# Two orders changed in the opening of a two-block transformer kernel: VectorE's first wait, and what TensorE does between two sets of transposes

## The reference, cut to what matters

```python
for l in range(DEPTH):                       # two layers
    h = rmsnorm(x, g_mix_pre[l])
    mk, mv = jnp.split(rmsnorm(mem, g_mem[l]) @ w_mem_kv[l], 2, axis=-1)
    ...
```

## Time and profile before

| | before |
|---|---|
| median of 3 runs | 2247.61 us (2244.99 to 2247.92) |
| the profiled execution's own time | 2242.63 us |
| its span, first to last instruction | 2241.2 us |
| TensorE, matmuls | 2093.4 us busy, 93% |
| VectorE | 1163.9 us busy, 52% |
| ScalarE | 867.2 us busy, 39% |
| GpSimd | 233.6 us busy, 10% |
| mean granted TensorE clock | 0.97 |

### The profile page before, as it was taken

One profiled execution on the slowest core, in us unless ns is written; L12 is line 12 of the kernel. 1 busy time (PEld: TensorE's weight loads), 2 busy tenths in 40 slices (PEclk: granted clock), 3 DMA queues, 4 the chain that ended last, 5 costly groups with the idle time before them and its releaser, 6 DMA issues.

```text
span 2241.2 us, 24583 instructions
## 1 busy us (share of the span) xinstructions
PE 2093.4 (93%) x9984; PEld 1703.9 (76%) x9984; DVE 1163.9 (52%) x2252; ACT 867.2 (39%) x1553; POOL 233.6 (10%) x161
## 2 busy tenths in 40 slices
PE   6988899999998899999999998999999799999787
PEld 6976688888786777688887888877777566877675
DVE  5325453333225756553333226998964528766553
ACT  5345443222124356532223122367552223256520
POOL 1000010000002000010000002677700000000000
PEclk9999899999999999999999999999999899999998
DMA  6320122232223112223222222222222222211211
GB/s 229 113 91 4 48 85 94 94 101 106 96 102 113 58 65 85 85 85 106 101 94 94 94 104 103 94 76 76 94 86 94 75 75 76 76 38 38 75 57 56
DMA packets 28800, 192.60 MB, mean 86 GB/s; under 512 B 3264, under 2 KB 3408, under 8 KB 7440
## 3 DMA queue, kind: packets, MB, share of 16 engines
q1 hardware_dynamic: 24848, 175.96, 22.5%
q0 software_dynamic: 3264, 12.99, 1.7%
q10 hardware_dynamic: 576, 2.10, 0.2%
HBM read 186.84 MB, written 4.19 MB: 85 GB/s over the span
## 4 chain that ended last, share of the span: by engine, by line
PE 79%; DVE 14%; ACT 5%; issue 1%; DMA 0%; POOL 0%; SPq 0%; DVEq 0%; ACTq 0%; POOLq 0%
PE bank L397 23%; PE bank L398 22%; PE bank L399 22%; DVE bank L2064 5%; PE bank L1750 2%; DVE WL L369 2%; PE bank L1738 1%; PE bank L1641 1%; ACT WH L355 1%; PE bank L1651 1%; PE bank L2205 1%; PE bank L1212 1%; DVE XL L558 1%; PE bank L1743 1%; PE bank L542 1%
## 5 line engine op out<-in xcount | busy, mean ns | idle before, releaser
L397 PE MATMUL bank<-XH,WH 128*128 128x512 f32 (+1 forms) x1504 | 597.1, 397 | 15.7 <-DVE XL L558 10.3
L399 PE MATMUL bank<-XH,WL 128*128 128x512 f32 (+1 forms) x1504 | 567.8, 378 | 0.0
L398 PE MATMUL bank<-XL,WH 128*128 128x512 f32 (+1 forms) x1504 | 567.2, 377 | 0.0
L369 DVE TENSOR_TENSOR WL<-RAW,WH 128x2048 fp32r<-128x2048 f32 x128 | 293.2, 2292 | 468.8 <-ACT WH L355 468.6
L355 ACT ACTIVATE WH<-RAW 128x2048 fp32r<-128x2048 f32 x148 | 282.2, 1908 | 342.2 <-PE bank L399 336.7
L397 PEld LDWEIGHTS bank<-XH,WH 128*128 128x128 f32 x1504 | 286.7, 191 | 85.4 <-issue 25.6
L398 PEld LDWEIGHTS bank<-XL,WH 128*128 128x128 f32 x1504 | 286.9, 191 | 55.1 <-issue 6.6
L399 PEld LDWEIGHTS bank<-XH,WL 128*128 128x128 f32 x1504 | 286.3, 190 | 53.5 <-issue 0.8
L2064 DVE SCALAR_TENSOR_TENSOR bank<-conv_in,cols,bank 128x512 f32<-128x512 f32 x290 | 198.2, 750 | 1.1
L397 PE MATMUL bank<-WH,XH 128*128 128x512 f32 (+2 forms) x416 | 158.3, 380 | 12.8 <-DVE XL L558 6.3
L398 PE MATMUL bank<-WL,XH 128*128 128x512 f32 (+2 forms) x416 | 154.4, 371 | 0.0
(11 more groups left out here) (325 smaller groups left out, 2934.1 us busy)
## 6 DMA issues: line engine op xcount, KB each, us to landing
RAW<-weights SPq DMA_DIRECT2D x164, 1024.0 KB, 4.9
row_a<-rows POOLq DMA_DIRECT2D x7, 512.0 KB, 5.7
row_b<-rows POOLq DMA_DIRECT2D x6, 512.0 KB, 6.0
x_res<-x SPq DMA_DIRECT2D x1, 2048.0 KB, 16.7
kv<-mem_park POOLq DMA_DIRECT2D x2, 1024.0 KB, 5.0
out<-x_res ACTq DMA_DIRECT2D x4, 512.0 KB, 2.6
mem_tok<-mem SPq DMA_DIRECT2D x1, 1024.0 KB, 4.9
mem_tok<-mem POOLq DMA_DIRECT2D x1, 1024.0 KB, 8.3
```

Of the source, the lines that this page charges most:

```text
L369: dve.tensor_tensor(WL[j][:, :], RAW[j][:, :], WH[j][:, :].bitcast(F32), ALU.subtract).then_inc(*lo.mark())
L397: pe.matmul(ps, ah, bh, start=first, stop=False)
L398: pe.matmul(ps, ah, bl, start=False, stop=False)
L399: return pe.matmul(ps, al, bh, start=False, stop=last)
```

## The change

Two waits or steps change their places; no instruction other than a semaphore wait is added or removed. TensorE multiplies layer 0's memory keys between the turns for layer 0 and those for layer 1, instead of after both. VectorE's wait for the small row stands ahead of the gate sums, not ahead of its first squares.

```diff
     def memory_keys_pe():
         PE.wait_ge(*after("constants"))
         PE.wait_ge(*after("m1_scaled"))
         turn_memory_pe("m1_0", mem_tok[0])
-        turn_memory_pe("m1_1", mem_tok[0])
         for layer in range(2):
             PE.wait_ge(*after("emptied", f"m1_{layer}", KB - 1))
             features_pe(M1 + 2 * layer, n=MEM, first=MEM * layer)
+            if layer == 0:
+                turn_memory_pe("m1_1", mem_tok[0])
             chunk_pe(M1 + 2 * layer + 1, ("mem_v", layer), 256, KB, MEMT, from_x, per_unit=KB, first=MEM * layer)
             for t in range(2 * layer, 2 * layer + 2):
                 turn_normed_pe(("n0",), t, True)
...
     def memory_keys_dve():
-        DVE.wait_ge(*after("small_rows"))
         m1 = mem_tok[0]
         DVE.wait_ge(*after("mem"))
         dve.tensor_tensor_reduce(row_b[:, :], m1[:, 0, :], m1[:, 0, :], 1.0 / D, 0.0, ALU.mult, ALU.add,
...
     def gate_sum_dve():
+        DVE.wait_ge(*after("small_rows"))
         for t in range(NT):
             DVE.wait_ge(*after("emptied", "in_a", 0, t))
```

## The result

| | before | changed |
|---|---|---|
| median of 8 runs | 2246.97 us | 2253.41 us (2249.07 to 2255.6) |
| ratio, 95% interval | | 1.0031 (1.002 to 1.0042) |
| the profiled execution's own time | 2242.63 us | 2253.7 us |
| its span | 2241.2 us | 2252.2 us |

The medians differ by 6.4 us (forecast: 6.2), the two profiled executions by 11.1. The opening of the changed kernel follows. First ScalarE's timeline; it answers to the earlier trace rows.

A forecast was written before the change was run, and what follows sets the result against it. TensorE was taken as the bound: the start of its unbroken work plus holes opened behind it. A 4.7 us later second product plus a 1.5 us slow stretch gave 2247.6 + 6.2 = 2253.8 us, range 2248.5 to 2258.

The forecast's parts named there:

- The first squares are worth nothing: VectorE's first squares start about 2.93 us earlier, worth 0, because units 0 and 1 wait for their DMAs.
- The row's DMA makes unit 1 late: GpSimd's 512 KB row, issued at about 7.9, makes weight unit 1 land 1.25 us later; bounds 0 and 1.25.
- The first product: TensorE's layer-0 key product starts at 21.5 instead of 24.22, takes 7.2 us and ends at 28.7.
- The turns behind it: Layer-1 turns occupy TensorE after the first product, from 28.7 to about 31.7, some 3.0 us.
- The chain on VectorE: From layer 1's first low part at 29.7, 13.95 us to unit 2's low half; second product +4.7 us.
- The slow stretch: After TensorE's 4.4 us wait, the second layer's product runs at half clock; 1.5 us, bounds 0 and 3.0.
- From the start of the second layer's product on, the two traces should differ by a constant.: Sign for everything behind the opening: later waits are relative to TensorE's stream, so nothing is given back.
- VectorE isn't late: Rival: unit 2 is ready when TensorE is, so TensorE's own order decides, +0.3 us; 7%.
- the change is faster: Rival: unit 2's low half is ready after the turns of x; -3.3 us, or -4.8 without the slow stretch; 5%.
- the extras don't come: Rival: VectorE's chain decides, but without slow stretch, late unit 1 or slow first-product matmuls; some +3.5 us; 23%.
- cheaper than two: Rival of two slow stretches: the first product runs slow for longer or the hole costs two; +7.7 to +9.2 us; 10%.
- the forecast's own range: Range given to the main forecast of +6.2 us: +4.7 to +7.5 us, at 55%.

The follow-up runs named there:

- the small row alone: Kernel before with only VectorE's wait for the small row moved to the gate sums, TensorE's order unchanged; ratio 1.0006 (0.9998 to 1.0015).
- the norms first: Changed kernel with ScalarE's squares and VectorE's norms of x ahead of their layer-1 parts; ratio 1.0016, timed again 1.0005.
- filling the wait: Changed kernel with 36 unread transposes of constants on TensorE ahead of the second layer's product; ratio 1.0016 (1.0008 to 1.0025).

## Why the prediction was right, step by step

- *The first squares are worth nothing.* Right: 2.90 us earlier, and unit 0's low half at the same time.
- *The row's DMA makes unit 1 late.* Forecast 1.25, measured 1.02 (0.97 with the small row alone). The row got 39.7% beside 57.8% of the weights' queue, and it landed at 15.9, behind unit 1 (15.3), so not all of it came first.
- *The first product.* Forecast start 21.5, measured 21.28; 7.53 us instead of 7.2 (by the same measure 7.35 in the kernel before, which the prediction read as 7.2). The prediction's reason, that TensorE comes out of a pause in both kernels, does not hold for the changed one: there the clock did not fall ahead of the product, it had not risen yet, and came up at 25.1 us. That the two costs are so close is luck.
- *The turns behind it.* Forecast 3.0 us, measured 2.83.
- *The chain on VectorE.* Forecast from 29.7 to 43.65, measured 29.73 to 43.42. The wait of TensorE: 4.4 and 4.09. The start of the second product: +4.7 and +4.48. Putting the norms first removes the wait and 5.5 of the 6.6 us, so this is shown, not only argued.
- *The slow stretch.* The mis-sized term: forecast 1.5 us by the 16 matmuls of the kernel before, measured 25 x 0.09 = 2.3, confirmed by filling the wait. The nearest row, a slow stretch from 24.2 to 27.6 us behind a pause of 1.9 us, was no measure for this one: behind the wait of 4.1 us the clock was down from 42.2 to 49.0, and the second product took 8.2 to 8.4 us in all four profiles that have the wait. The errors of the first terms and this one nearly cancel: 6.2 against 6.6 in the opening. That the medians come within 0.2 us of the forecast is luck; the same two kernels timed again differ by 7.0.
- *"From the start of the second layer's product on, the two traces should differ by a constant."* This failed. The slow stretch itself lies behind that start and takes the difference from 4.48 to 6.6 us, by the prediction's own sum; and 4.4 us came on top between 59 and 350 us. From there to the end it held for the first profile (11.0 and 11.0), not for the second (11.1 and 12.7). I compared a forecast with a median and so did not need it; from the two profiled executions alone one would have put the loss at 11 us.
- *Rivals.* That VectorE isn't late, and that the change is faster, fell with the wait. That the extras don't come fell with rows of both: unit 1 was late, and the clock did fall. The slow stretch was dearer than one and cheaper than two (2.3 us against 1.5 and 3.0), and the sum stayed in the forecast's own range. In the rival of a faster kernel the 4.8 us count the old slow stretch twice, since the 5.8 us of its sum already leave it out, and the 2.0 us for the turns stand against 3.0 in the forecast and 2.83 measured.

## What to carry to other kernels

Work that an engine does in another's shadow belongs to the order as much as the work on the path: moving eight groups of turns behind a product moved 13.7 us of VectorE's list (29.73 to 43.42), and only 9.7 us of TensorE's work (to 39.38) lay between to hide it. Before reordering the bound engine, walk the other engines' lists from the moved step to the next thing that the bound engine needs; if they hold unrelated work, move that first: the squares and norms moved here gave back 5.5 us of the opening. One swapped step on VectorE, with TensorE's order left alone, took 3.6 us out of the opening, and with twelve idle transposes 4.5 us off the median. A wait that is taken away early also releases what is queued behind it on another engine: here a DMA that delayed the transfer of unit 1 by 1.0 us.

## What the runs showed of the hardware that I had not expected

The granted clock listed for the opening does not always fit the matmuls. In the changed kernel the first product's matmuls are 0.21 us apart until 25.07 us, but the clock is listed at 1.00 throughout, as in this stretch (7 of them in 1.52 us):

```profile
20.90:22.80 1.90, 1.52 (x7) 1.53 (x8) 1.90 (x2) 0.00 (x0) 0.00 (x0) 1.00 0.78 323
```

A trace's clock records begin with a rise, and the time ahead of it is listed at 1.00: at 25.1 us in the changed kernel, 27.4 with the norms first, 20.8 in the kernel before. The distance between matmuls is the surer sign. And the same first product took 7.53 us in the changed kernel and 8.54 with the norms first, with the same list on TensorE up to its end and the same start (21.28 and 21.24): 1.0 us that no instruction of TensorE's explains. The clock does: it rose at 25.1 us in the one and at 27.4 in the other, and 2.3 us with matmuls 0.21 us apart in place of 0.12 are 1.0 us. What sets the moment is not shown. The 1.0 us is as much as the DMA term under study, which is why the two units' distance had to carry that verdict, and not the time.
